# Nine groups of identity products dropped between the items of two attention layers

## What is computed

```python
def reference(x, positions, ...):
    h = x
    for layer in range(2):
        h = h + hybrid_mixer(rms_norm(h, attn_norm[layer]), positions, layer, ...)
        hn = rms_norm(h, ffn_norm[layer])
        if layer == 0:
            h = h + swiglu(hn, dense_w_gate, dense_w_up, dense_w_down)      # width 3584
        else:
            h = h + moe_ffn(hn, router, moe_w_gate, moe_w_up, moe_w_down)   # 8 experts, top 2
    return rms_norm(h, final_norm)
```

## Time and profile before

| | us |
|---|---|
| three timed runs | 1490.77, 1493.33, 1492.91 |
| median | 1492.91 |
| the profiled execution's own time | 1494.18 |
| its span, first to last instruction | 1492.4 |
| PE busy in the span | 1466.8 (98%) |
| DVE busy | 1226.7 (82%) |
| ACT busy | 1026.5 (69%) |
| mean granted clock of TensorE | 0.997 |

### The profile page before, as it was taken

How to read it: one execution, slowest core, us unless ns; L and a number is a source line. 1 busy time by engine, 2 the same in 40 slices (tenths; PEclk the granted TensorE clock), 3 DMA queues, 4 the chain that set the end, 5 groups by cost and what they waited for, 6 DMA issues and landing times.

```text
span 1492.4 us, 18656 instructions
## 1 busy us (share of the span) xinstructions
PE 1466.8 (98%) x7020; PEld 1219.2 (82%) x7020; DVE 1226.7 (82%) x1499; ACT 1026.5 (69%) x1356; POOL 109.8 (7%) x185
## 2 busy tenths in 40 slices
PE   8999999999999999999999999999999999999996
PEld 8787888888888888888888888888888888888885
DVE  6787565555687799998999898898998998998896
ACT  7475544444457577787888787787787788778774
POOL 2540000000153100000000000000000000000020
PEclk9999999999999999999999999999999999999999
DMA  7324654544431389999999999999999999999992
GB/s 268 109 118 153 235 197 170 204 191 139 139 120 62 128 332 378 359 380 379 378 361 396 355 366 381 372 356 383 381 365 380 383 374 370 372 375 390 406 401 105
DMA packets 46317, 436.85 MB, mean 293 GB/s; under 512 B 4113, under 2 KB 10641, under 8 KB 22033
## 3 DMA queue, kind: packets, MB, share of 16 engines
q1 hardware_dynamic: 43488, 427.48, 73.9%
q0 software_dynamic: 1584, 5.77, 1.0%
q10 hardware_dynamic: 1152, 2.37, 0.5%
HBM read 430.88 MB, written 4.72 MB: 292 GB/s over the span
## 4 chain that ended last, share of the span: by engine, by line
PE 88%; DVE 6%; DMA 2%; ACT 2%; POOL 1%; issue 1%; POOLq 0%; ACTq 0%; SPq 0%; DVEq 0%
PE pair L948 48%; PE work L948 30%; PE work L920 3%; DVE w_lo L1681 3%; PE pair L1018 2%; PE pair L920 1%; DMA ring<-in_moe_w_down 1%; PE work L1092 1%; PE work L935 1%; ACT w_hi L1318 1%; DMA ring<-in_moe_w_gate 1%; PE work L1226 1%; POOL rope_s L768 0%; DVE arena L1751 0%; DVE hidT_lo L1995 0%
## 5 line engine op out<-in xcount | busy, mean ns | idle before, releaser
L1681 DVE TENSOR_TENSOR w_lo<-ring,w_hi 128x1024 fp32r<-128x1024 f32 (+2 forms) x810 | 957.4, 1215 | 179.9 <-ACT w_hi L1318 170.2
L1318 ACT ACTIVATE w_hi<-ring 128x1024 fp32r<-128x1024 f32 (+2 forms) x810 | 831.1, 1051 | 313.4 <-PE pair L948 112.0
L948 PE MATMUL pair<-w_hi,hnT_hi 128*128 128x512 f32 x672 | 265.2, 395 | 3.4 <-issue 1.7
L948 PE MATMUL pair<-w_hi,hnT_lo 128*128 128x512 f32 x672 | 262.0, 390 | 0.0
L948 PE MATMUL pair<-w_lo,hnT_hi 128*128 128x512 f32 x672 | 261.5, 389 | 0.0
L948 PE MATMUL work<-w_hi,hidT_hi 128*128 128x512 f32 x552 | 215.2, 390 | 2.7 <-DVE hidT_lo L1995 1.6
L948 PE MATMUL work<-w_lo,hidT_hi 128*128 128x512 f32 x552 | 214.8, 389 | 0.0
L948 PE MATMUL work<-w_hi,hidT_lo 128*128 128x512 f32 x552 | 214.8, 389 | 0.0
L948 PE MATMUL pair<-w_hi,xU_hi 128*128 128x512 f32 x448 | 177.1, 395 | 0.0
L948 PE MATMUL pair<-w_hi,xU_lo 128*128 128x512 f32 x448 | 174.8, 390 | 0.0
L948 PE MATMUL pair<-w_lo,xU_hi 128*128 128x512 f32 x448 | 174.3, 389 | 0.0
(11 more groups left out here) (243 smaller groups left out, 1305.8 us busy)
## 6 DMA issues: line engine op xcount, KB each, us to landing
ring<-in_moe_w_gate SPq DMA_DIRECT2D x56, 2048.0 KB, 9.8
ring<-in_moe_w_up SPq DMA_DIRECT2D x56, 2048.0 KB, 9.9
ring<-in_moe_w_down SPq DMA_DIRECT2D x56, 2048.0 KB, 9.7
ring<-in_dense_w_gate SPq DMA_DIRECT2D x7, 2048.0 KB, 7.5
ring<-in_dense_w_up SPq DMA_DIRECT2D x7, 2048.0 KB, 7.4
ring<-in_dense_w_down SPq DMA_DIRECT2D x7, 2048.0 KB, 7.4
ring<-in_w_in SPq DMA_DIRECT2D x4, 2048.0 KB, 7.8
ring<-in_w_out SPq DMA_DIRECT2D x4, 2048.0 KB, 10.2
```

Source lines behind the costliest of these rows:

```text
L948: mm = pe.matmul(b, lhs[x_part][k + kk], w[w_part][:, kk, :], start=(first and kk == 0 and i == 0), stop=(last and kk == 1 and i == 2))
L1318: return act.activation(o, i, ACT.Copy)
L1681: dve.tensor_tensor(lo, raw, hi.bitcast(F32), ALU.subtract).then_inc(lo_done, 1)
```

## The change

The nine `FL` items are taken out of the two lists. Nothing else is changed: the order of all other items stays, and so do the four groups ahead of the first layer and the code that would handle an `FL` item.

```diff
 LISTS = ("""
-X.0.0 X.0.1 SP.0 N1.0 SP.1 SP.2 SP.3 FL.2 X.1.0 X.1.1 PC.0 SP.4 ...
+X.0.0 X.0.1 SP.0 N1.0 SP.1 SP.2 SP.3 X.1.0 X.1.1 PC.0 SP.4 ...
...
-TP.mla.1.3 U.dsa.1.0 U.dsa.1.1 O.diff.1.0 CB.mla.1.3 TP.diff.1.1 U.diff.1.3 CB.dsa.1.1 FL.9 CB.dsa.1.0 O.mla.1.3
+TP.mla.1.3 U.dsa.1.0 U.dsa.1.1 O.diff.1.0 CB.mla.1.3 TP.diff.1.1 U.diff.1.3 CB.dsa.1.1 CB.dsa.1.0 O.mla.1.3 TP.dsa.1.0
...
-D2.1 SP.24 SP.25 SP.26 WO.0.0 SP.27 OT.1.1 OT.1.0 WO.0.1 WO.1.0 SP.28 SP.29 NF1.0 XF.0.0 SP.30 WO.1.1 XF.0.1 NF1.1
-FL.13
+SP.25 SP.26 WO.0.0 SP.27 OT.1.1 OT.1.0 WO.0.1 WO.1.0 SP.28 SP.29 NF1.0 XF.0.0 SP.30 WO.1.1 XF.0.1 NF1.1
 """, """
...
-O.diff.1.1 U.dsa.1.1 D2.0 FL.5 TP.diff.1.0 O.dsa.0.0 U.diff.1.2 TP.dsa.1.0 CB.dsa.1.1 CB.diff.1.2 CB.dsa.1.0 OT.0.1
-OT.0.0 SP.22 O.diff.1.0 SP.23 U.diff.1.3 CB.diff.1.3 O.dsa.1.0 TP.dsa.1.1 SP.24 TP.diff.1.2 WO.0.0 O.dsa.1.1 SP.25
-TP.diff.1.3 SP.26 O.diff.1.2 D1.1 SP.27 D2.1 O.diff.1.3 WO.0.1 OT.1.0 OT.1.1 NF1.0 FL.7 XF.0.1 NF2.0 XF.0.0 HS.0.0
-HS.0.1 WO.1.0 RT.0 SP.28 SP.29 SP.30 WO.1.1 XF.1.0 FL.8 XF.1.1 NF1.1 PL.0 FL.10 FL.11 NF2.1 RT.1 HS.1.0 FL.12 GR.0.0
-PL.1 HS.1.1 GR.0.1 GR.1.0 GR.1.1
+O.diff.1.1 U.dsa.1.1 D2.0 TP.diff.1.0 O.dsa.0.0 U.diff.1.2 TP.dsa.1.0 CB.dsa.1.1 CB.diff.1.2 CB.dsa.1.0 OT.0.1 OT.0.0
+SP.22 O.diff.1.0 SP.23 U.diff.1.3 CB.diff.1.3 O.dsa.1.0 TP.dsa.1.1 SP.24 TP.diff.1.2 WO.0.0 O.dsa.1.1 SP.25
+TP.diff.1.3 SP.26 O.diff.1.2 D1.1 SP.27 D2.1 O.diff.1.3 WO.0.1 OT.1.0 OT.1.1 NF1.0 XF.0.1 NF2.0 XF.0.0 HS.0.0 HS.0.1
+WO.1.0 RT.0 SP.28 SP.29 SP.30 WO.1.1 XF.1.0 XF.1.1 NF1.1 PL.0 NF2.1 RT.1 HS.1.0 GR.0.0 PL.1 HS.1.1 GR.0.1 GR.1.0
+GR.1.1
 """)
```

More of the change, by code:

```diff
@@ L37 @@
 LISTS = ("""
-X.0.0 X.0.1 SP.0 N1.0 SP.1 SP.2 SP.3 FL.2 X.1.0 X.1.1 PC.0 SP.4 SP.5 SP.6 N1.1 SP.7 SP.8 SP.9 AN SP.10 C1.0 PC.1 PI.1
-TR C1.1 C2.0 SP.11 R.kr.0 PI.0 SP.12 PK.0 SP.13 PK.1 CT.0 SP.14 IT.0 R.kr.1 SP.15 SP.16 PA.1 C2.1 KIT.0 KIT.1 QC.0.0
+X.0.0 X.0.1 SP.0 N1.0 SP.1 SP.2 SP.3 X.1.0 X.1.1 PC.0 SP.4 SP.5 SP.6 N1.1 SP.7 SP.8 SP.9 AN SP.10 C1.0 PC.1 PI.1 TR
+C1.1 C2.0 SP.11 R.kr.0 PI.0 SP.12 PK.0 SP.13 PK.1 CT.0 SP.14 IT.0 R.kr.1 SP.15 SP.16 PA.1 C2.1 KIT.0 KIT.1 QC.0.0
 QC.0.1 IT.1 KV.0.1 U.idx.1.0 U.idx.1.1 U.idx.0.0 KV.0.0 U.idx.0.1 U.idx.1.2 R.i.0 R.i.1 MR U.idx.1.3 U.idx.0.2 SP.17
@@ L48 @@
 TP.dsa.0.0 U.mla.1.3 O.diff.0.0 CB.diff.1.0 TP.diff.1.2 U.diff.1.1 O.dsa.0.0 TP.diff.1.0 D1.0 CB.diff.1.1 O.diff.1.2
-TP.mla.1.3 U.dsa.1.0 U.dsa.1.1 O.diff.1.0 CB.mla.1.3 TP.diff.1.1 U.diff.1.3 CB.dsa.1.1 FL.9 CB.dsa.1.0 O.mla.1.3
-TP.dsa.1.0 D2.0 O.diff.1.1 CB.diff.1.3 OT.0.0 TP.dsa.1.1 OT.0.1 O.dsa.1.0 D1.1 TP.diff.1.3 O.dsa.1.1 O.diff.1.3 SP.23
-D2.1 SP.24 SP.25 SP.26 WO.0.0 SP.27 OT.1.1 OT.1.0 WO.0.1 WO.1.0 SP.28 SP.29 NF1.0 XF.0.0 SP.30 WO.1.1 XF.0.1 NF1.1
-FL.13
+TP.mla.1.3 U.dsa.1.0 U.dsa.1.1 O.diff.1.0 CB.mla.1.3 TP.diff.1.1 U.diff.1.3 CB.dsa.1.1 CB.dsa.1.0 O.mla.1.3 TP.dsa.1.0
+D2.0 O.diff.1.1 CB.diff.1.3 OT.0.0 TP.dsa.1.1 OT.0.1 O.dsa.1.0 D1.1 TP.diff.1.3 O.dsa.1.1 O.diff.1.3 SP.23 D2.1 SP.24
+SP.25 SP.26 WO.0.0 SP.27 OT.1.1 OT.1.0 WO.0.1 WO.1.0 SP.28 SP.29 NF1.0 XF.0.0 SP.30 WO.1.1 XF.0.1 NF1.1
 """, """
```

## The result

The changed kernel is slower. The median of nine runs is 1497.10 us against 1492.66 us for nine of the kernel before; the ratio is 1.0026, with a 95% interval from 1.0017 to 1.0034. Measured again on another occasion, eleven runs against 27, it was 1495.38 against 1492.52, ratio 1.0018 (1.0009 to 1.0027). So the loss by the medians is 2.9 to 4.4 us, where I had forecast none. (The ratios are not exactly those of the medians: 1497.10 / 1492.66 would be 1.0030.) The profiled execution took 1497.10 us and its span is 1495.3 us, 2.9 us more than before, as its own time is (1497.10 - 1494.18).

A forecast was written before the change was run, and what follows sets the result against it. PE, busy 98% of the span, was taken to bound the kernel; gains of 0.05, 0.05 and up to 0.1 us were taken as 0.1, so 1492.91 - 0.1 = 1492.8 us, range 1490.3 to 1496.3.

The forecast's parts named there:

- The sum of 0.1 us: Over all nine groups: 0.05 at FL.5, 0.05 at FL.10 and FL.11, up to 0.1 at FL.12; 0.1 us gain taken.
- The idle stretches it named: PE idle behind dropped groups grows, gaining nothing: 1.83 us before the first gate product, about 1.0 before tile 1's output product.
- held to 515.13 by DVE: Router product behind FL.10 and FL.11 waits for DVE's columns until 515.13, so dropping the pair gains 0.05 us.
- the chance of the clock: Identity products hold and raise PE's clock; nine fewer can let it fall, at 1.7 us of PE's time per fall.
- falls at 142 and near 517: Clock falls at the dense stage, up to 1.7 us, or in the gathering, 0.7 us after slack; one fall, chance 0.2.
- falls in two places: Clock falls at 142 and late in layer 1's last stretch, 1.7 us each: 1496.2 us, chance 0.09.
- no fall: The main forecast: no measurable change, 1492.8 us, chance 0.62.
- its 0.05 us: At FL.5, 476.10 us: the products behind wait for DVE and ACT, so dropping it gains only 0.05 us.
- In this start it is paid already: Half clock between 11.40 and 15.20 us already costs the 1.7 us of one fall before the change.
- One fall: One more clock fall, at 142 or near 517: 0.7 to 1.7 us, time 1493.5 to 1494.5, chance 0.2.
- the groups were on PE's path: All nine groups delay PE: up to 4.45 us gained, 1488.5 us; chance 0.09.

## Why the prediction was wrong

**The gain.** The sum of 0.1 us came from asking, at each group, what the next PE instruction waits for. The idle stretches it named came out: 1.82 us before the first gate product (1.83 forecast), 0.97 before the output product of tile 1 (1.0), both released as before. The groups were worth nothing as work on PE's path, and dropping them freed nothing. Two readings were off, neither at a cost. Behind FL.2 the turns of the second tile could start only 0.59 us earlier (7.82 against 8.41), after 0.39 us of waiting for the load of `x`, so the idle stretch there became 2.55 and not 2.8 us. And the router product behind FL.10 and FL.11 was not held to 515.13 by DVE: it needs only the first of the two DVE operations to start. Without the last four groups it starts 0.84 us behind the start of that pair (514.76 against 513.92), before 1.44 us (515.18 against 513.74). The 0.6 us gained there are worth nothing in front of the experts, since DVE's next steps, up to 518 us, stand at the same distances as before.

**The step that failed** is the chance of the clock. The forecast put the falls that the nine groups had prevented at nothing: its sum of 1492.8 us has no term for them. The prediction had read from the start that identity products raise and hold the clock, and it was right to trust the row: without the last four groups the clock fell at the end of layer 1 in all three profiles, with them in none of eleven. The Trainium skill (TensorE: Matmul & The Clock Gate, Part 4: PE-mode transpose) says that turns don't engage the full clock. The groups are such turns, and by the three profiles against the eleven they do hold it here. The prediction listed falls at 142 and near 517 as rivals and gave falls in two places 1496.2 us, with a chance of 0.09, against 0.62 for no fall. The falls came in those two places in the profile, and the medians are 1495.4 and 1497.1 us. Its terms were not quite those: it had 1.7 us for each fall and nothing for the start, and the profile shows 1.78, 0.58 and 1.07, with the first expert product back at full clock; that 1.7 + 1.7 comes out near the measured time is in part luck. Three things made the chance too small:

- *One execution was read as all.* Idle stretches of 1.39 and 1.03 us left the clock at 1.00 in the trace of before, and I took this for a property of their lengths. The runs here show no such property: 1.83 us held the clock in four profiles with FL.13 dropped and let it fall in two, and 2.40 us held it in the start of the kernel without FL.5. A single trace gives no chance for this; its absence in one execution says little.
- *The search went by idle time.* FL.5 stands in a stretch in which PE is busy without a gap, so I asked only for its 0.05 us. Without it the clock fell there in two profiles, with 0.33 us of idle PE ahead of the fall, and where that could be priced it cost 1.7 us. The products around it are short and narrow (64 to 256 columns, turns among them).
- *The start was counted as paid.* "In this start it is paid already" held for one execution. Without FL.2 the half clock lasted to 17 us in two of six profiles, and the first gate product was 1.07 and 1.11 us later in these; with FL.2 it never lasted as long. FL.2 and FL.13 cost 1.4 us as a pair and nothing that can be told alone; why the pair costs more is open.

**The sizes.** One fall was priced at 0.7 to 1.7 us, and that was about right: the profiles show 1.78 at 143 and 1.7 at 477. At the last stretch, where slack takes part of it, they show 0.58 and 1.26 us behind half clocks of twice the length, and 0 with half of that stretch's groups. The pair (1.4), FL.5 (0.7), FL.7 and FL.9 (0.2) and the last four (1.6) add up to 3.9 us, within the 2.9 to 4.4 of the whole; with 1.3 us of uncertainty on each, that is no more than agreement.

**The rivals.** That the groups were on PE's path is out: without them the kernel is slower. That one fall would come, and be partly paid for by slack, was true of the last stretch alone.

## What to carry to other kernels

Work whose result nobody reads can still be worth its place: before taking it out, look at the granted clock and at what PE streams around it, and not only at who waits for whom. Ask also in stretches where PE is busy without a gap, as around FL.5, and not only at idle ones; the length of an idle stretch told little here. And where the loss comes in some executions only, one trace of before that shows no fall is weak evidence that none will come; eleven runs with the clock of each told more than any single profile.

## What the hardware showed that I had not expected

Sixteen rows of ordinary products of 8 columns kept PE busy for 1.79 us, twice as long as eight turns of 128 columns, 0.11 us for each of either, and with them in place PE's clock fell at 477 and at 518 us with PE busy throughout. An idle stretch of 2.40 us left the clock up in one profile, one of 1.83 us let it fall in another. A half clock from 517 to 520 us cost nothing, one from 518 to 525 us cost 1.26 us at the same place. And the clock of the start was down until 15, 16 or 17 us, or not at all, from one execution to the next of nearly the same program.
